# The first 50 microseconds of a decoder layer on one core: who splits, who squares, and how the norm is taken

## The reference

```python
def rmsnorm(x, g):
    xf = x.astype(jnp.float32)
    y = xf * lax.rsqrt(jnp.mean(xf * xf, axis=-1, keepdims=True) + EPS)
    return (y * g.astype(jnp.float32)).astype(x.dtype)

z = rmsnorm(h, g_mix) @ w_in          # 2048 -> 5120: q, k, v, u, vc
...                                   # per-head norms, attention, chunk MLP
h = h + o @ w_out                     # output projection
h = h + (jax.nn.silu(f @ w_gate) * (f @ w_up)) @ w_down
h = h + jax.nn.sigmoid(rmsnorm(h, g_ple) @ w_ple_gate) * (p @ w_ple_proj)
```

## Time and profile before

| | |
|---|---|
| time, median of 3 runs | 2538.48 us (2538.07 to 2540.17) |
| the profiled execution's own time | 2537.53 us |
| its span, first to last instruction | 2535.8 us |
| granted TensorE clock, mean over the span | 0.994 |
| TensorE busy | 2492.0 us (98%) |
| VectorE busy | 1452.1 us (57%) |
| ScalarE busy | 1014.6 us (40%) |
| GpSimd busy | 235.1 us (9%) |
| moved by transfers | 368.58 MB |

### The profile page before, as it was taken

How to read it: one execution, slowest core, us unless ns; L and a number is a source line. 1 busy time by engine, 2 the same in 40 slices (tenths; PEclk the granted TensorE clock), 3 DMA queues, 4 the chain that set the end, 5 groups by cost and what they waited for, 6 DMA issues and landing times.

```text
span 2535.8 us, 47986 instructions
## 1 busy us (share of the span) xinstructions
PE 2492.0 (98%) x20428; PEld 2469.4 (97%) x20428; DVE 1452.1 (57%) x1588; ACT 1014.6 (40%) x1351; POOL 235.1 (9%) x266
## 2 busy tenths in 40 slices
PE   6998999999999998999999999999999999999999
PEld 6998999999999998999999999999999999999999
DVE  6368776554446468555555555555555555557433
ACT  4333233333433364444444444444444444445221
POOL 4000111011101220000000000000000000003000
PEclk9999999999999999999999999999999999999999
DMA  4245665554432442454545454545444554445322
GB/s 184 101 159 191 242 217 215 184 192 142 161 116 101 159 152 100 138 130 140 128 141 126 142 126 142 126 142 126 142 126 142 126 143 125 143 125 201 137 98 85
DMA packets 73343, 368.58 MB, mean 145 GB/s; under 512 B 9658, under 2 KB 9658, under 8 KB 45378
## 3 DMA queue, kind: packets, MB, share of 16 engines
q1 hardware_dynamic: 50994, 285.29, 31.7%
q0 software_dynamic: 22016, 80.42, 15.0%
q10 hardware_dynamic: 144, 0.01, 0.0%
HBM read 305.98 MB, written 59.70 MB: 144 GB/s over the span
## 4 chain that ended last, share of the span: by engine, by line
PE 92%; DVE 6%; DMA 1%; issue 1%; ACT 0%; SPq 0%; DVEq 0%; ACTq 0%
PE out_ps L1954 27%; PE out_ps L1737 22%; PE pair_ps L1969 12%; PE mix_ps L1969 10%; PE out_ps L1969 7%; PE tok_ps L1969 5%; PE out_ps L1859 4%; PE pair_ps L1776 1%; DVE x_lo L1269 1%; DVE w_lo L1260 1%; DVE op_lo L1627 1%; DVE dot_s L1292 1%; DVE k_ring L1291 1%; PE tok_ps L1844 0%; DMA k_ring<-cache_k 0%
## 5 line engine op out<-in xcount | busy, mean ns | idle before, releaser
L1737 PE MATMUL out_ps<-x_hi,w_hi 128*128 128x260 f32 x1792 | 382.1, 295 | 20.3 <-DVE w_lo L1260 10.5
L1522 DVE TENSOR_TENSOR w_lo<-w_raw,w_hi 128x1024 fp32r<-128x1024 f32 x196 | 238.9, 1223 | 234.7 <-ACT w_hi L1041 234.7
L1737 PE MATMUL out_ps<-x_hi,w_lo 128*128 128x260 f32 x1792 | 363.7, 285 | 0.0
L1737 PE MATMUL out_ps<-x_lo,w_hi 128*128 128x260 f32 x1792 | 363.0, 284 | 0.0
L1737 PEld LDWEIGHTS out_ps<-x_hi,w_hi 128*128 128x128 f32 x1792 | 281.2, 191 | 24.8 <-DVE w_lo L1260 9.4
L1954 PE MATMUL out_ps<-act_hi,w_hi 128*128 128x260 f32 x1400 | 281.7, 282 | 0.0
L1954 PE MATMUL out_ps<-act_lo,w_hi 128*128 128x260 f32 x1400 | 280.8, 282 | 0.0
L1954 PE MATMUL out_ps<-act_hi,w_lo 128*128 128x260 f32 x1400 | 280.3, 281 | 0.0
L1737 PEld LDWEIGHTS out_ps<-x_hi,w_lo 128*128 128x128 f32 x1792 | 279.1, 190 | 0.0
L1737 PEld LDWEIGHTS out_ps<-x_lo,w_hi 128*128 128x128 f32 x1792 | 278.8, 190 | 0.0
L1041 ACT ACTIVATE w_hi<-w_raw 128x1024 fp32r<-128x1024 f32 x196 | 205.4, 1052 | 141.7 <-PE out_ps L1954 75.5
(11 more groups left out here) (247 smaller groups left out, 5505.9 us busy)
## 6 DMA issues: line engine op xcount, KB each, us to landing
w_raw<-w_units SPq DMA_DIRECT2D x155, 1024.0 KB, 4.8
w_extra<-w_units SPq DMA_DIRECT2D x50, 1024.0 KB, 4.8
h_dram<-staging POOLq DMA_DIRECT2D x80, 520.0 KB, 5.6
k_ring<-cache_k SPq DMA_DIRECT2D x50, 512.0 KB, 5.1
v_ring<-cache_v POOLq DMA_DIRECT2D x43, 512.0 KB, 4.9
acc<-cache_v POOLq DMA_DIRECT2D x21, 512.0 KB, 4.8
k_third<-cache_k SPq DMA_DIRECT2D x14, 512.0 KB, 4.4
h<-x_t SPq DMA_DIRECT2D x4, 1040.0 KB, 10.5
```

The costliest lines, as they stand in the source:

```text
L1522: dve.tensor_tensor(half_slot(w_lo, job), src, half_slot(w_hi, job), ALU.subtract)\
L1737: mm = pe.matmul(out_ps[:, 2 * (t % 2) + a, 0:HALF], w[:, u % 2, cols], x[:, a * HALF:(a + 1) * HALF], start=first and n == 0, stop=last a ...
```

## The change

Several edits, all in the first 50 us:

- GpSimd no longer squares, adds or makes low parts. It builds the constants and waits for the loads.
- ScalarE takes all 16 squares, after unit 1's split; VectorE adds all of them, and makes the low parts that GpSimd made.
- `x_r` is exp(-0.5 * ln(mean + eps)), both on ScalarE; VectorE's reciprocal goes. The function table for log and exp is set up at the start.
- The first two blocks of unit 0's weights (`FIRST_COLS`, 256 columns) are a load of their own, issued by ScalarE ahead of the gain, and are split by themselves; the other six of the half come next. The x pieces are two tiles each up to tile 8; the second half of unit 0's weights is loaded behind the third piece and split after tile 5.
- TensorE does 20 products of `ones` by `ones` (`WARM_UP`) before the input is there. Their result isn't used.
- The sum over the partitions stands at block 14 of unit 1 instead of 12.

```diff
-X_PIECES = [0, 2, 4, 8, 12, 16]
-POOL_SQUARES = 6
-X_SQUARES = KT - POOL_SQUARES
-POOL_LO = 2
+X_PIECES = [0, 2, 4, 6, 8, 12, 16]
+X_SQUARES = KT
+FIRST_COLS = 2 * P
+WARM_UP = 20
...
             load_x(0)
             half = SLOTS * P // 2
-            sp.dma_start(w_raw[:, 0, 0:half], w_units[0, :, 0:half]).then_inc(w_in_first, 16)
+            sp.dma_start(w_raw[:, 0, FIRST_COLS:half], w_units[0, :, FIRST_COLS:half]).then_inc(w_in_half, 16)
             load_x(1)
+            load_x(2)
             sp.dma_start(w_raw[:, 0, half:], w_units[0, :, half:]).then_inc(w_in[0], 16)
-            for i in range(2, len(X_PIECES) - 1):
+            for i in range(3, len(X_PIECES) - 1):
                 load_x(i)
...
-            pool.wait_ge(x_in[0], 16)
-            square_input(0)
-            low_w(0, 1)
-            pool.wait_ge(x_in[1], 16)
-            square_input(1)
-            square_input(2)
-            square_input(3)
-            pool.wait_ge(x_in[2], 16)
-            square_input(4)
-            low_w(1, 1)
-            square_input(5)
...
         def _(act):
+            act.dma_start(w_raw[:, 0, 0:FIRST_COLS], w_units[0, :, 0:FIRST_COLS]).then_inc(w_in_first, 16)
             act.dma_start(gain_mix[:, :], g_mix).then_inc(gain_in, 16)
...
-            act.wait_ge(built, 1)
-            act.activation(y[:, 0, 0:1], one[:, 0:1], ACT.Copy)
+            load_ln_exp()
...
                 split(x_hi[:, k, :], h[:, k, :], gain_mix[:, k:k + 1])
+                if k == 0:
+                    act.wait_ge(w_in_first, 16)
+                    act.activation(w_hi[:, 0, 0:FIRST_COLS], w_raw[:, 0, 0:FIRST_COLS], ACT.Copy)\
+                        .then_inc(first_hi_done, 1)
                 if k == 1:
-                    act.wait_ge(w_in_first, 16)
-                    high_w(0, 0)
-                if k == 3:
+                    act.wait_ge(w_in_half, 16)
+                    act.activation(w_hi[:, 0, FIRST_COLS:8 * P], w_raw[:, 0, FIRST_COLS:8 * P], ACT.Copy)\
+                        .then_inc(hi_done, 1)
+                if k == 5:
                     act.wait_ge(w_in[0], 16)
                     high_w(0, 1)
             split_w(1)
-            for k in range(POOL_SQUARES, KT):
+            for k in range(KT):
                 act.activation(x_sq[:, k, :], h[:, k, :], ACT.Square).then_inc(sq_done, 1)
             split_w(2)
-            chained(act.activation(y[:, 0, 1:2], one[:, 0:1], ACT.Sqrt))
             act.wait_ge(built, 2)
-            root(0, D_MODEL, x_r[:, :])
-            load_ln_exp()
+            act.wait_ge(x_sum_ready, 1)
+            act.activation(halves(x_r[:, :]), pair, ACT.Ln, bias=eps[:, 0:1], scale=1.0 / D_MODEL)\
+                .then_inc(root_done, 1)
+            act.wait_ge(root_done, 1)
+            act.activation(x_r[:, :], x_r[:, :], ACT.Exp, scale=-0.5).then_inc(x_r_ready, 1)
...
                 low_x(k, h[:, k, :], gain_mix[:, k:k + 1])
+                if k == 0:
+                    dve.wait_ge(first_hi_done, 1)
+                    dve.tensor_tensor(w_lo[:, 0, 0:FIRST_COLS], w_raw[:, 0, 0:FIRST_COLS], w_hi[:, 0, 0:FIRST_COLS],
+                                      ALU.subtract).then_inc(first_lo_done, 1)
                 if k == 1:
-                    low_w(0, 0)
+                    dve.wait_ge(hi_done, 1)
+                    dve.tensor_tensor(w_lo[:, 0, FIRST_COLS:8 * P], w_raw[:, 0, FIRST_COLS:8 * P],
+                                      w_hi[:, 0, FIRST_COLS:8 * P], ALU.subtract).then_inc(lo_done, 1)
+                if k == 6:
+                    low_w(0, 1)
             low_w(1, 0)
-            first = POOL_SQUARES
-            for k in range(first + 2, KT, 2):
-                dve.wait_ge(sq_done, k + 2 - first)
-                chained(dve.tensor_tensor(x_sq[:, first:first + 2, :], x_sq[:, first:first + 2, :],
-                                          x_sq[:, k:k + 2, :], ALU.add))
-            chained(dve.tensor_tensor(x_r[:, :], x_sq[:, first, :], x_sq[:, first + 1, :], ALU.add))
-            dve.wait_ge(pool_sum_done, 1)
-            chained(dve.tensor_tensor(x_r[:, :], x_r[:, :], x_sq[:, 0, :], ALU.add), sum_done)
+            low_w(1, 1)
+            for k in range(2, KT, 2):
+                dve.wait_ge(sq_done, k + 2)
+                chained(dve.tensor_tensor(x_sq[:, 0:2, :], x_sq[:, 0:2, :], x_sq[:, k:k + 2, :], ALU.add))
+            chained(dve.tensor_tensor(x_r[:, :], x_sq[:, 0, :], x_sq[:, 1, :], ALU.add), sum_done)
             low_w(2, 0)
             low_w(2, 1)
-            dve.wait_ge(built, 2)
-            invert(0, x_r[:, :])
+            dve.wait_ge(x_r_ready, 1)
...
+            pe.wait_ge(ones_built, 1)
+            for n in range(WARM_UP):
+                pe.matmul(pair_flat[:, 0:P], ones[:, :], ones[:, :], start=True, stop=True)
             unit(0, 1, in_operand, each=lambda b: pe.wait_ge(x_lo_done, b + 1))
...
                 if u == 1:
-                    between[12] = lambda: sum_features(x_r, sum_done, 1, (root_done, 1))\
+                    between[14] = lambda: sum_features(x_r, sum_done, 1, (root_done, 1))\
                         .then_inc(x_sum_ready, 1)
```

More of the change, by code:

```diff
@@ L442, in build @@
         built = sem("built")
-        pool_lo_done = sem("pool_lo_done")
-        pool_sum_done = sem("pool_sum_done")
+        x_r_ready = sem("x_r_ready")
+        first_hi_done = sem("first_hi_done")
+        first_lo_done = sem("first_lo_done")
+        ones_built = sem("ones_built")
         pool_step = sem("pool_step")
@@ L485, in load_unit @@
             def load_unit(u):
[L487 to L491, removed]
+                if u >= 2:
+                    sp.wait_ge(lo_done, 2 * u - 2)
                 src = w_units[u] if u < U_FFN else w_units[U_PROJ + u - U_FFN]
@@ L586, in after_low @@
             def after_low(job, it=0):
-                sp.wait_ge(lo_done, it * CHUNK_JOBS + (JOB0 + job + 1 - POOL_LO))
+                sp.wait_ge(lo_done, it * CHUNK_JOBS + (JOB0 + job + 1))
             def after_sums(pair, it=0):
@@ L683, in chained @@
                 pool.wait_ge(pool_step, steps[0])
-            chained(pool.memset(ones[:, :], 1.0))
+            pool.memset(ones[:, :], 1.0).then_inc(ones_built, 1)
+            pool.wait_ge(ones_built, 1)
             chained(pool.memset(eps[:, :], EPS))
@@ L1525, in after_low @@
             def after_low(job, it=0):
-                dve.wait_ge(lo_done, it * CHUNK_JOBS + (JOB0 + job + 1 - POOL_LO))
+                dve.wait_ge(lo_done, it * CHUNK_JOBS + (JOB0 + job + 1))
             def low_raw(job, i, half, it=0):
@@ L1747, in unit @@
                 for b in range(SLOTS):
-                    if b % 8 == 0 and u >= 2:
-                        pe.wait_ge(lo_done, 2 * u + b // 8 + 1 - POOL_LO)
-                    elif b % 8 == 0:
-                        pe.wait_ge(pool_lo_done if b else lo_done, u + 1)
+                    if u == 0 and b == 0:
+                        pe.wait_ge(first_lo_done, 1)
+                    elif b % 8 == 0 or u == 0 and b == FIRST_COLS // P:
+                        pe.wait_ge(lo_done, 2 * u + b // 8 + 1)
                     if b in between:
@@ L1944, in after_low @@
             def after_low(job, it=0):
-                pe.wait_ge(lo_done, it * CHUNK_JOBS + (JOB0 + job + 1 - POOL_LO))
+                pe.wait_ge(lo_done, it * CHUNK_JOBS + (JOB0 + job + 1))
             def plain_block(job, b, tile, hi, lo, first, last):
```

1 line of the change is left out of this document (added).

## The result

The changed kernel takes 2523.26 us (median of 4 runs, 2521.89 to 2524.75), against 2538.28 for the kernel before, run beside it (4 runs, 2537.31 to 2540.17). The ratio is 0.994, with a 95% interval of 0.9923 to 0.9957: 15.0 us or 0.6% faster. The forecast was 2524.7 within 2521 to 2529.

What follows compares the result with a forecast made beforehand. TensorE's own time bounds the kernel, plus start-up waits for VectorE, slowed by GpSimd. Unit 2 starting 12.96 us earlier plus 0.85 from the clock gives 13.8: 2538.48 to 2524.7 us, range 2521 to 2529.

Steps and rivals of the forecast that it cites:

- VectorE without GpSimd: Units 0 and 1: `x_lo` fall from 1.63 to about 0.7 us each; TensorE enters unit 1 at 22.4 against 34.86.
- rival 3: VectorE's slowness comes from ScalarE or transfers, not GpSimd; TensorE 6.5 us later, 2545.0 us; chance 0.01.
- Squares on ScalarE, adds on VectorE, the select: Norm's sum: VectorE's adds, 9.55 us, set the pace; GpSimd's select costs 0.95 (0 to 1.5); sum ready at 34.8.
- Log and exp: Norm ahead of unit 2: 3.57 us from sum to unit 2; root and reciprocal take 4.2 in place of 1.5.
- First weight piece, gain behind it: Start of unit 0: ScalarE starts about 5.3 to 5.5, block 0 at 7.5 against 9.4; hidden, otherwise worth 1.9 us.
- Loads: Input loads for units 0 and 1: same bytes reordered, landings taken as unchanged; 0.5 us later is the other bound.
- Warm-up: Before block 0: 20 products end between 6 and 12 us; cost or saving lies within TensorE's slack, costed at nothing.
- Sum at block 14: Unit 1: TensorE waits 2.4 us for the sum at block 14; two blocks earlier only shortened that wait.
- The clock: Unit 2's start: the fall after the wait, 1.7 us lost before, may go or stay; half taken, 0.85 gained.
- rival 1: Clock falls in the wait ahead of the sum; unit 2 starts at 39.6, 2525.5 us; chance 0.13.
- Rival 2: ScalarE and VectorE miss their dates through late loads or the select; unit 2 at 41 to 42, 2528.5 us; chance 0.08.
- Rival 4: After unit 2's start: later waits give the gain back, all of it lost being 2538.5 us; chance 0.04.

Runs made afterwards that it cites:

- Run 1: Kernel before with only GpSimd's squares, adds and low halves moved to ScalarE and VectorE; old loads, root and reciprocal, block 12, no warm-up: 2527.16 us.
- Runs 3 and 4: Changed kernel with GpSimd given extra work on its own zero buffer: fourteen multiplies that read (2534.49 us), or 32 memsets that only write (2523.75 us).
- run 10: Changed kernel with GpSimd's select put behind VectorE's first tile, and ScalarE not waiting for it before the norm: 2523.91 us.
- run 2: Kernel before with only log and exp in place of root and reciprocal, and the function table's first setting changed: 2533.28 us.
- run 6: Changed kernel with the old loads: old x pieces, no 256-column first weight piece, gain first, old split order: 2525.65 us.
- run 5: Changed kernel without warm-up, 0 products of constants instead of 20: 2523.15 us.
- run 8: Changed kernel with the sum over partitions back at block 12 of unit 1 instead of 14: 2525.19 us.
- run 11: Changed kernel with the gain's load issued ahead of the first weight piece on ScalarE's queue: 2526.6 us.

## Why the prediction was right

*VectorE without GpSimd.* Right in mechanism and dates: splits of unit 1 at 21.40 (21.15 forecast), sum at 34.45 (34.8). Run 1 shows that the moved work alone gives 10.2 of the 15 us. Runs 3 and 4 show that GpSimd's reads slow VectorE, and not its being busy, ScalarE or the transfers; this rules out rival 3.

*Squares on ScalarE, adds on VectorE, the select.* VectorE set the pace. The select held it 0.77 us, for which 0.95 was taken, and without it there the start came 0.7 earlier (run 10).

*Log and exp.* From the sum's being ready to unit 2 the path took 37.99 - 34.45 = 3.54 us, 3.57 forecast. In the kernel before these two functions alone give 4.0 us (run 2). The two later switches of the function table were costed at nothing; no run tests them by themselves.

*First weight piece, gain behind it.* Wrong in the gain's date: it was taken to land by 5.5 at the latest and was waited for until 7.07. Behind the weight piece it took 5.7 us from issue to landing, alone in front 3.9. Block 0 started at 9.06 instead of 7.5, hardly before the old 9.4. The cover named for it held: unit 2's start didn't move.

*Loads.* Costed at nothing by name; they are worth 0.3 to 0.8 us of unit 2's start (run 6). The term speaks only of tiles 6 and 7 and of ScalarE. The dates for VectorE, however, contain the gain: an `x_hi` 6 that is ready at 13.05, with ten `x_lo` left, supposes that tiles 4 and 5 came earlier and were split in the 2.3 us in which VectorE had idled. With the old pieces its `x_lo` 4 starts only at 13.37 (run 6). So the dates held, and the sentence that priced the loads at nothing didn't.

*Warm-up.* Nothing either way, as forecast (run 5). The 20 products took 7.07 us, and their end at 8.3 is within the bounds of 6 and 12. For the later bound the forecast has block 7 at 17.6; from its own 0.72 a block it is 12 + 7 x 0.72 = 17.0, which changes nothing, as both lie within the wait.

*Sum at block 14.* Costed at nothing, since it only shortened a wait. By position alone that is nearly right (0.3, run 8). Run 8 shows 1.6 us more, since the clock fell behind the longer wait, and blocks 12 to 15 at that clock set unit 2's start.

*The clock.* The term that was mis-sized: half of 1.7 was taken as gained, and the fall behind unit 2's start went whole, 1.5 by the mixing product. The start was 13.4 earlier for 13.0 forecast. Together this is 14.9 there, 14.7 by the span and 15.0 by the medians, for 13.8 forecast.

That the forecast and not rival 1 came true is in part luck. The wait at the sum, taken as 2.4, was 1.44: the sum was ready 0.35 earlier than forecast, and TensorE reached block 14 some 0.5 later. Behind it the sum's matmuls took 1.14, at full clock. With the same instructions and only two loads exchanged (run 11), the wait was 1.80 and the clock fell. It then moved unit 2 by 0.5, less than the 1.2 that rival 1 had. The rows of the kernel before didn't tell which of the two would come.

*Rival 2.* The sum came 0.35 earlier than forecast, so it didn't occur. The loads can be late all the same: between profiles of the same loads the sum's date moved by up to 0.5 us.

*Rival 4.* The gain isn't given back: the distance from unit 2's start to the end shrank by 1.3 us.

## What to carry to other kernels

Where an engine's instructions take twice their price, look at what the neighbour engine does in the same microseconds, and move the neighbour's reads before anything is made faster: here that alone was worth 10 of 15 us. Follow a start-up path on the engine that ends it, with its idle times, since pieces that come earlier count only there. Where TensorE must wait, price the clock behind the wait on its own line, and put the wait behind as much ready work as there is.
